# Hybrid decoder trunk on one core: the eight attention heads of a layer as one unrolled stream, with the next head prepared in pieces inside the present one

## The reference, cut to what matters

```python
def _diff_attn(q, k, v, lam_vecs, gain, lam_init, pos, valid):
    q = _rope(_to_heads(q, 2 * DA_HEADS), pos) ...   # k the same
    ...
        s = jnp.einsum('bhcqd,bhckd->bhcqk', qi, k) * scale
        p = jax.nn.softmax(jnp.where(mask, s, NEG), axis=-1)
        w = p[:, :, 0] - lam * p[:, :, 1]
        return jnp.einsum('bhqk,bhkv->bhqv', w, v)
    o = _rmsnorm(o, gain) * (1.0 - lam_init)

def _fox_attn(q, k, v, fz, bias, gain, valid):
    D = jnp.cumsum(jax.nn.log_sigmoid(fz + bias), axis=1)
    ...
        s = jnp.einsum('bhqd,bhkd->bhqk', qi, k) * scale
        s = s + di[..., :, None] - D[:, :, None, :]
        p = jax.nn.softmax(jnp.where(mask, s, NEG), axis=-1)
        return jnp.einsum('bhqk,bhkv->bhqv', p, v)
    return _rmsnorm(o, gain)
```

## Time and profile before

| | us |
|---|---|
| median of three runs | 4075.69 (4073.25 to 4076.86) |
| profiled execution: its own time / its span | 4074.96 / 4073.1 |
| TensorE busy, with weight loads beside it | 3361.2 / 2123.9 |
| VectorE / ScalarE busy | 1681.9 / 756.1 |

### The profile page before, as it was taken

The page is one execution under the profiler, slowest core; times in us unless marked ns, Lnnn a source line. Parts: engine busy times, 40 slices in busy tenths (PEclk is TensorE's granted clock), DMA queues, the critical chain, the costliest instruction groups (busy, mean ns, idle before and its releaser), DMA issues.

```text
span 4073.1 us, 44633 instructions
## 1 busy us (share of the span) xinstructions
PE 3361.2 (83%) x15000; PEld 2123.9 (52%) x15000; DVE 1681.9 (41%) x2185; ACT 756.1 (19%) x1686; POOL 121.3 (3%) x131
## 2 busy tenths in 40 slices
PE   6999877777788399999859998777677884999994
PEld 3666445555544255555436664455455442555552
DVE  4777333334423322323267773333344233223324
ACT  2222123222111011111122221232221110111111
POOL 2100000000000100000000000000000001000001
PEclk9999977768899699999969999777688996999997
DMA  8400100000100799999820001000001007999996
GB/s 255 128 21 10 42 6 5 5 5 11 47 3 0 272 408 409 411 410 410 316 97 21 21 10 42 6 5 5 8 9 47 3 0 279 408 408 409 410 410 263
DMA packets 140729, 614.74 MB, mean 151 GB/s; under 512 B 13432, under 2 KB 47736, under 8 KB 122744
## 3 DMA queue, kind: packets, MB, share of 16 engines
q1 hardware_dynamic: 104664, 495.88, 30.9%
q0 software_dynamic: 16944, 60.89, 4.6%
q10 hardware_dynamic: 19056, 57.16, 3.8%
HBM read 538.33 MB, written 75.56 MB: 151 GB/s over the span
## 4 chain that ended last, share of the span: by engine, by line
PE 75%; DVE 8%; issue 6%; DMA 5%; ACT 3%; POOL 1%; ACTq 1%; DVEq 1%; SPq 0%; POOLq 0%
PE ps L924 13%; PE ps L1054 6%; PE ps L1147 6%; PE ps L1247 6%; PE ps L1237 6%; PE ps L1004 6%; PE ps L1206 5%; PE ps L1212 4%; PE ps L971 4%; PE ps L1105 3%; PE ps L1264 3%; PE ps L1069 3%; DMA arena<-xg 3%; PE ps L993 2%; DVE negmax L1448 1%
## 5 line engine op out<-in xcount | busy, mean ns | idle before, releaser
L924 PE MATMUL ps<-arena 128*128 128x512 f32 (+3 forms) x1632 | 548.6, 494 | 43.0 <-DMA arena<-w_in 22.2
L924 PEld LDWEIGHTS ps<-arena 128*128 128x128 f32 (+1 forms) x1632 | 267.2, 189 | 327.9 <-issue 313.6
L1004 PE MATMUL ps<-arena 128*65 128x128 f32 (+2 forms) x1440 | 280.1, 339 | 66.2 <-ACT arena L664 27.3
L971 PE MATMUL ps<-rounded 128*128 128x512 f32 (+4 forms) x600 | 212.1, 470 | 107.4 <-DVE rounded L1436 54.3
L1448 DVE TENSOR_REDUCE negmax<-ps 16x1 f32<-16x16 f32 (+8 forms) x216 | 151.6, 705 | 281.2 <-PE ps L976 280.9
L1004 PEld LDWEIGHTS ps<-arena 128*65 128x65 f32 (+1 forms) x1440 | 194.9, 170 | 129.8 <-issue 92.2
L1206 PE MATMUL ps<-arena 128*128 128x512 f32 x560 | 253.5, 606 | 2.6 <-ACT arena L846 2.6
L1147 PE MATMUL ps<-arena 128*128 128x512 f32 (+1 forms) x576 | 252.1, 596 | 0.0
L1054 PE MATMUL ps<-arena 128*128 128x256 f32 (+1 forms) x1152 | 251.6, 380 | 0.0
L1247 PE MATMUL ps<-arena 128*64 128x256 f32 x2240 | 249.5, 381 | 0.0
L1212 PE MATMUL ps<-arena 128*128 128x256 f32 x1120 | 247.4, 379 | 0.0
(11 more groups left out here) (295 smaller groups left out, 3937.1 us busy)
## 6 DMA issues: line engine op xcount, KB each, us to landing
arena<-w SPq DMA_DIRECT2D x210, 2048.0 KB, 12.9
xg<-arena POOLq DMA_DIRECT2D x51, 512.0 KB, 12.2
arena<-xg ACTq DMA_DIRECT2D x39, 512.0 KB, 10.2
xg<-arena ACTq DMA_DIRECT2D x35, 512.0 KB, 7.6
arena<-w_in SPq DMA_DIRECT2D x16, 1024.0 KB
arena<-xg ACTq DMA_DIRECT2D x35, 256.0 KB, 11.1
xg<-arena ACTq DMA_DIRECT2D x70, 128.0 KB, 9.4
arena<-w_in SPq DMA_DIRECT2D x16, 512.0 KB, 4.1
```

The source lines that it names most:

```text
L924: mm = pe.matmul(dst[0:hi - lo, a:b], w[:, k, lo:hi], uT[:, k, a:b], start=(k == 0), stop=(k == KD - 1))
L971: mm = pe.matmul(flat[0:r, side + x:side + y], q[:, cols(j)], k[:, x:y], start=(i == 0), stop=False, skip_group_check=True)
L1004: mm = pe.matmul(flat[0:AW + 1, pv_at(j, a.maps):pv_at(j, a.maps) + r], Vh[0:rows(i), i, :], WT[0:rows(i), g % 3, n * P:n * P + r], start= ...
```

## The change

- **One stream.** The loops over heads and the `meet` between phases 2 and 3 go: units (head, tile, map) of all eight heads are numbered through, and scores are issued ahead across the boundary of two heads. The code is written out for eight heads (a layer's loop remains): on TensorE 3134 instructions stand in the program where there were 1573.
- **Pieces.** The preparation of head n + 1 is cut into thirds of the tokens (352, 352, 336 columns) and into kinds: a projection, b permutation and rotary passes, c to f the four selection groups. Tables (`DURING_DA`, `DURING_FX`) put each piece into one of three slots of a query tile of head n, on all three engines; head 0's go between the matmuls of the value projection (`DURING_V`). All pieces share PSUM bank 2, and each waits until the one before it is copied out. A differential head has 18 pieces, a forgetting head three (a0 to a2).
- **Value products.** The turned weights stay in the array (128 columns) and 64 value columns stream past; the result is 128 x 64, already the right way round, so the ones column, the final transposes and the per-head copy of the values go. ScalarE divides by the row sum as it copies. All results lie in bank 7, and a tile's first product waits for the copy of the tile before.
- **The rest.** The forget gates are projected first, in two column groups that write to different PSUM partitions; the tables are loaded in another order and the value projection waits for them; the heads' weights have two buffers (in `mix`) and the first two are loaded during phase 1; decay rows of all four heads are fetched at once; squares and norm of head n are done on VectorE in tiles 0 and 1 of head n + 1.

```diff
+CUTS = [(0, 352), (352, 704), (704, L)]
+DURING_DA = {(0, 0): "a0", (0, 2): "b0", (1, 0): "a1", (1, 1): "c0", (1, 2): "d0", (2, 0): "e0", (2, 1): "f0",
...
+DURING_FX = {(0, 0): "a0", (1, 0): "a1", (2, 0): "a2"}
...
+            def piece_pe(layer, n, piece):
...
+                for semaphore, value in bank2:
+                    pe.wait_ge(semaphore, value)
+                bank2.clear()
+                if kind == "a":
...
+                    for k in range(KD):
+                        mm = pe.matmul(out, w_qk[b][:, k, :], uT[:, k, lo:hi], start=(k == 0), stop=(k == KD - 1))
+                    mm.then_inc(t_proj, 1)
...
+                    pe.matmul(out, sel[:, 2 * g, :], xh[:, 0:hi - lo], start=True, stop=False)
+                    pe.matmul(out, sel[:, 2 * g + 1, :], xl[:, 0:hi - lo], start=False, stop=True).then_inc(t_rep, 1)
...
-                        mm = pe.matmul(flat[0:AW + 1, pv_at(j, a.maps):pv_at(j, a.maps) + r], Vh[0:rows(i), i, :],
-                                       WT[0:rows(i), g % 3, n * P:n * P + r], start=(i == 0), stop=(i == j),
+                        mm = pe.matmul(ps[0:r, 7, at:at + AW], WT[0:rows(i), g % 3, m * P:m * P + r],
+                                       V[0:rows(i), i, n * AW:(n + 1) * AW], start=(i == 0), stop=(i == j),
                                        skip_group_check=True)
...
+                for t in range(TILES):
+                    n, j = divmod(t, T)
+                    new = ahead(t)
+                    late = new[1:] if n < HEADS and j == T - 2 else []
+                    for u in new[:len(new) - len(late)]:
+                        scores(u)
+                    piece_pe(layer, n + 1, piece_at(n, j, 0))
+                    if t:
+                        outputs(t - 1, len(bundles((t - 1) % T)) - 1)
+                    turn_weights(t, 0)
+                    piece_pe(layer, n + 1, piece_at(n, j, 1))
+                    for b in range(1, len(bundles(j))):
+                        turn_weights(t, b)
+                        outputs(t, b - 1)
+                    for u in late:
+                        scores(u)
+                    piece_pe(layer, n + 1, piece_at(n, j, 2))
...
+            def attend_act(layer):
...
+                    new = ahead(t)
+                    if new:
+                        exps(new[0])
+                    if t:
+                        copy_out(t - 1)
+                    if n < HEADS:
+                        turned(t, 0)
+                    piece_act(layer, n + 1, piece_at(n, j, 0))
+                    for u in new[1:]:
+                        exps(u)
+                    piece_act(layer, n + 1, piece_at(n, j, 1))
...
+            def attend_dve(layer):
...
+                    new = ahead(t)
+                    if new:
+                        peak(new[0])
+                    if n < HEADS:
+                        join(t)
+                    else:
+                        v.wait_ge(t_P, ONE + U0 + LAST[t] + 1)
+                        v.reciprocal(rinv[0:rows(j), 2 * j:2 * j + 1], rowsum[0:rows(j), 2 * j:2 * j + 1]).then_inc(t_W, 1)
+                        turned(t, 0)
+                    for u in new[1:]:
+                        peak(u)
+                    piece_dve(layer, n + 1, piece_at(n, j, 0))
...
+                    for k in range(KD):
+                        for c in range(2):
+                            mm = pe.matmul(ps[64 * c:64 * c + HEADS, 0, :], w_ff[:, k, :],
+                                           uT[:, k, 512 * c:512 * c + 512], start=(k == 0), stop=(k == KD - 1))
...
+                            if k == KD // 2 - 1:
+                                piece_pe(layer, 0, DURING_V.get((j, 0)))
```

More of the change, by code:

```diff
@@ new lines, in build @@
+        DK = rounded[:, at:at + L]
+        at += 2 * wide + 8 * P
+        causal_r, ident_r = (rounded[:, at + i * P:at + (i + 1) * P] for i in range(2))
+        at += 2 * P
+        dh, dl = (rounded[0:HEADS, at + i * L:at + (i + 1) * L] for i in (1, 2))
+        assert at + 3 * L == ROUNDED
+        s = Place(SCRATCH + at)
+        powers = [s.take(L) for _ in range(3)]
+        ffx = powers[0][0:HEADS]
+        raw, rot = s.take(wide), s.take(wide)
+        V = s.take(T, 2 * HEADS * AW)
+        WT = s.take(3, 512)
@@ L275, in build, with weights_in @@
[L275 to L282, removed]
+        w_ff = s.take(KD, HEADS)
+        fx_c = s.take(1 + 1 + HEADS)
+        ah = [s.take(T, AW), s.take(T, AW)]
+        w_qk = [mix[:, 0:KD, D - 2 * P + b * P:D - P + b * P] for b in range(2)]
+        def weights_in(n, j, c):
+            if n < HEADS:
+                return powers[2] if c else powers[(n * T + j) % 2]
+            return powers[(0, 2, 1)[(n * T + j - HEADS * T) % 3]]
@@ new lines, in attend_pe @@
+            def attend_pe(layer):
+                U0, G0, J0 = layer * len(UNITS), layer * TURNS, layer * TILES
+                def scores(u):
+                    n, j, c = UNITS[u]
+                    r, wide_, side, ops = rows(j), META + P * j, side_of(u, j), operands_of(n)
+                    if j == 0 and c == 0:
+                        pe.wait_ge(t_qa, ONE + layer * QA[ALL] + QA[n + 1])
+                        pe.wait_ge(t_qd, ONE + layer * QD[ALL] + QD[n + 1])
+                    if n == HEADS and j == 0:
+                        pe.wait_ge(t_dk, ONE + layer * 3 + 3)
+                    if j == T - 1 and c == 0 and n + 1 < ALL:
+                        for semaphore, value in bank2:
+                            pe.wait_ge(semaphore, value)
+                        bank2.clear()
+                    if u >= 2:
+                        pe.wait_ge(t_P, ONE + U0 + u - (0 if j == T - 1 and c == 1 else 1))
+                    pairs_ = [(ops[2 * c], ops[2 * c + 1])] if n < HEADS else \
+                        [(ops[0], ops[1]), (ops[0], ops[2]), (ops[3], DK)]
+                    for x, y in pieces(side, wide_):
+                        for i, (q, k) in enumerate(pairs_):
@@ L1685, in _ @@
+                    attend_dve(layer)
+                    ats.end()
+                    meet(v, layer, 2)
                     meet(v, layer, 3)
@@ L1950, in constants @@
     c["c_sel"] = sel
+    fx_c = np.zeros((P, 2 + HEADS), f)
+    for n in range(HEADS):
+        fx_c[32 * n:32 * n + 2, 0] = 1
+        fx_c[32 * n + 2:32 * n + 4, 1] = -1
+        fx_c[32 * n:32 * n + 4, 2 + n] = -1
+    c["c_fx"] = fx_c
     swap = np.zeros((P, P), f)
```

661 lines of the change are left out of this document (337 added, 324 removed).

## The result

| | before | after |
|---|---|---|
| median of the runs, us | 4075.24 | 4007.07 (4000.33 to 4013.45, 4 runs) |
| ratio to before | | 0.9833 [0.9811, 0.9854] |
| profiled execution, its span, us | 4074.96, 4073.1 | 4012.46, 4010.6 |
| granted clock over the span | 0.884 | 0.865 |
| attention stage of a layer, us | 712.3 | 679.4 |

The account below looks back on a forecast made before the run. TensorE was taken as the bound in differential main parts, mostly busy at half pace. Front, heads and end summed to 551.5 us a layer against 712.3, saving 322 over two layers: 3754 us, range 3625 to 3890.

Parts of the forecast that it names:

- front: Layer's start before the heads: idle, gate weights, gates, values, head 0's pieces and waits, 114 us against 92.6 before.
- heads 0 to 2: First three differential heads: 24.1 us own work, 20.0 pieces, 13 waits, 5 clock loss; 62 each, 186 a layer.
- heads 4 to 6: Forgetting heads with a successor: 26.4 us own work, 14.0 pieces, 9 waits, 2.5 clock loss; 52 each, 156.
- The work: TensorE's full-clock time per head, main part plus pieces: 24.1 + 20.0, head 3 24.1 + 14.0, forgetting 26.4 + 14.0 us.
- The waits: TensorE's gaps in the new order, old ones, uncovered ones and bank 2: 13 us in heads 0 to 2, otherwise 9.
- rival C: Pieces in heads 0 to 6 stop the stream, each bank 2 wait costing a ScalarE queue round: 4110 us, chance 0.04.
- D: Whole program: forecast with code streamed at a price, 20 waits of 1 us a layer, 3794 us; forecast with it 0.52.
- I take 5 us of loss a head: Clock loss in differential heads, range 0 to 20 us; full clock to tile 4, flicker in tiles 5 to 8.
- Rival B: Clock stays low outside projection pieces in the heads: saving 51 us a layer, 3974 us; chance 0.26 including what lies towards it.
- The value products themselves: A head's 90 value records: nothing saved, 0.105 us each at full clock, twice that at half.
- full clock up to tile 4: Differential heads: projection pieces in tiles 0, 1 and 3 keep the clock full that far; tiles 5 to 8 flicker.
- The gates: Forget-gate projection in the front: kept at 14.3 us; the skill's column-group rule would give some 7.5.

Follow-up runs that it names:

- the fastest run here: Kernel after with 128 streamed columns, forgetting-head projection pieces in tiles 1, 3 and 5, and differential-head pieces issued later: 3898.77 us, ratio 0.9569.

## Why the prediction was wrong

By its own terms, a layer, measured in the windows shown first (work is covered time by the clock of the window, so the split is good to a few us):

| term | forecast | measured | of which work, waits, clock |
|---|---|---|---|
| front | 114 | 108.8 | gates 10.2 us for 14.3 |
| heads 0 to 2 | 186: 132.3, 39, 15 | 261.7 | 140.7, 51.7, 69.3 |
| head 3 | 52: 38.1, 9, 5 | 75.2 | 39.6, 13.3, 22.3 |
| heads 4 to 6 | 156: 121.2, 27, 7.5 | 193.5 | 123.6, 24.2, 45.7 |
| head 7 and end | 43.5 | 40.2 | |
| sum | 551.5 | 679.4 | |

- **The work was right.** In full-clock time heads 0 to 6 did 303.9 us of it against 291.6.
- **The waits were nearly right.** 89 us against 75, though not where they were expected. In heads 4 to 6 bank 2 makes 9.8 us of the 24 and ScalarE's copy of the output 11.4. In heads 0 to 3 the waits at permutation and selection pieces come to 24 us of the 65; waits for exponentials ahead of the scores and for the join ahead of the turning make 33 (total us, times, longest):

```profile
PE ps L1044 <- ACT arena L702: 16.7, 9, 2.5
PE ps L1069 <- DVE arena L1549: 16.4, 14, 1.6
PE ps L1015 <- ACT rounded L683: 9.7, 12, 1.1
```

  Nothing stopped the stream; rival C was far off, and no row asks for D.
- **The step that failed is the clock.** "I take 5 us of loss a head (0 to 20 ...), for a forgetting head 2.5." It measured 23 us a head in heads 0 to 2, 22 in head 3 and 15 in heads 4 to 6: 137 us a layer against 27.5. That is 110 of the 128 us that the layer missed. The row of before had 17 us of such loss in a differential head (42.28 x 0.41), and the forecast cut it to 5 because three dense pieces would hold the clock up; that reason failed. The turned form is the smaller part of the miss. The run is 253 us over the forecast; with the products in the old form it would still be 213 over, with 128 columns 179, and the fastest run here 145. Rival B, with 0.26, had the mechanism (74.5, 68 and 66 us for the three kinds of head; measured 87, 75 and 64.5; its head 7, at 49, was wrong, measured 35.3) and even one of the reasons, "the value products now stream half the columns", but I let it stand as a remark and priced the form of the product by its own duration alone.
- **The value products themselves** were priced rightly, and this misled me. At full clock they start 0.112 us apart, as before, and nothing is saved. At half clock they start 0.213 apart, the twice 0.105 of the prediction: the loads stretch with the clock (192 and 333 ns), and the up to 9 us a head for the case that they don't did not come. An instruction that costs the same by itself made all its neighbours slower: with 128 columns the transposes of the same kernel fell from 358 to 319 ns in the mean and the scores' records from 468 to 419.
- **Dense pieces do not carry the clock far.** I expected full clock up to tile 4 because projection pieces stand in tiles 0, 1 and 3. In differential head 1 the projection pieces stand at 632.7 to 647.1 and at 661.1 to 667.1 us. The windows right behind them are at 0.50 already, and so are 27 us on end, 22 of them covered, whose last three stand in the next head's first piece:

```profile
636.50:649.50 13.00, 10.56 (x41) 6.41 (x39) 5.13 (x12) 4.03 (x15) 0.00 (x0) 1.00 0.00 1
650.00:661.00 11.00, 8.56 (x27) 6.33 (x27) 5.72 (x12) 2.31 (x7) 0.00 (x0) 0.50 0.01 1
670.50:683.50 13.00, 11.62 (x39) 9.45 (x40) 4.61 (x9) 3.44 (x9) 0.00 (x0) 0.50 0.01 4
697.70:724.70 27.00, 21.95 (x86) 18.50 (x86) 7.29 (x16) 7.47 (x20) 0.00 (x0) 0.50 0.00 0
```

  The Trainium skill (TensorE: Matmul & The Clock Gate, Why this matters for your kernels) asks for no long idle gaps of TensorE between bursts. The kernel after keeps to that in heads 4 to 6, where the longest wait is 1.71 us, and has 0.73 there: here that advice was not enough.
- **The gates.** By the Trainium skill's rule on column groups (TensorE: Matmul & The Clock Gate, Part 3), two such matmuls run at the same time; the prediction's estimate from it was some 7 us less. The trace agrees with the rule:

```profile
452.68 9.99 PE L1186 MATMUL ps<-arena 128*4 128x512 f32 x32 [13.03 <-DMA arena<-w_in]
```

  Its records start in pairs 3 to 7 ns apart, and the pairs 0.847 us apart up to 458.7, where the clock goes from half to full, and 0.426 after. At full clock the 16 pairs are 6.8 us; one by one, as before, 32 records of that spacing are 13.6 (with 16 short ones 14.28). Half clock at the start, after 13.03 us of idling, ate about half of that gain.

What stays open: which property of the stream the clock goes by (the value products changed the columns alone, the added selecting products and the turning by products also the number of records and loads); what holds the clock down in heads 0 to 3, where neither the old form nor 128 columns alone brought head 1 above 0.72 in the first layer, and no kernel brought any head above 0.89; why head 7, with the same 64-column products and no dense pieces, stands at 0.84 where heads 4 to 6 stand at 0.73; and why the same form costs 112 us in the old order and 40 in the new one.

## What to carry to other kernels

A product's form has a second price besides its duration: what it streams can move the clock at which its neighbours run. Before exchanging stationary and moving operand, compare the moving columns per load, and where the clock is already below 1 take a shorter stream for a likely loss and time it. Where TensorE is at half clock, work may be free: streaming 128 columns instead of 64 gained 74 us here, and with the dense pieces spread over the head as well, the kernel takes 3900 us (0.9584 of before). That holds only below full clock: in the front, where it was nearly full, added records cost their time, and with 256 columns in heads 0 to 3 they cost more than the clock gave back. In a forecast of overlap start from the clock of the window, then look at its gaps; a loss that the clock has in a row of before should be dropped only for a reason that a row shows.

## What the hardware showed unexpectedly

- Turned value products, new order: 64, 128 and 256 streamed columns give a clock of 0.65, 0.70 and 0.78 in head 1; in head 5 64 and 128 give 0.74 and 0.94.
- Adding 48 records of selecting products, 352 or 336 columns each, to head 1 left its length unchanged (85.3 and 85.4 us), clock 0.70 to 0.84; the same records in the front cost 6.8 us.
- Turning by two product records instead of one transpose record shortened head 5 from 64.6 to 57.2 us and lengthened head 1 from 88.8 to 92.5.
- The load of 128 columns for 64 moving ones takes 192 ns at full clock and 333 at half (medians of two windows); the load of 65 columns runs from 128 to 236.
- Two projections of 4 rows, in column groups at partitions 0 and 64, ran side by side: the records start in pairs, a pair every 0.426 us at full clock.
